# A weight chunk's split put behind the softmax pieces, and large VectorE pieces cut up

## The reference, cut to what matters

```python
for l in range(DEPTH):                       # DEPTH = 2
    shift, scale, gate = jnp.split(sc @ w_ada[l] + b_ada[l], 3, axis=-1)
    h = rms(x, norm_w[l]) * (1.0 + scale[:, None]) + shift[:, None]
    ...
    u = h @ w_in
    qa, ka, va, qb, kb, vb, cq, ckv, kpe, z = jnp.split(u, split_points(), axis=-1)
    ...                                      # rms of q and k per head, rotation of qb, kb
    o_a = natten_latent(qa, ka, va, ka_c, va_c, rpb_a[l])
    o_b = swa_latent(qb, kb, vb, kb_c, vb_c, sink_b[l])
    o_c = mla_latent(qc, kc, vc, kc_c, vc_c)
    x = x + gate[:, None] * merge_out(o_a, o_b, o_c, z, w_out[l])
```

## Time and profile before

| | |
|---|---|
| median of 3 runs | 3752.88 us (3751.07 to 3753.28) |
| profiled execution | 3745.93 us |
| its span | 3744.1 us |
| PE busy | 3560.6 us, 95% |
| DVE, ACT busy | 2012.7 us (54%), 1673.0 us (45%) |
| granted clock of TensorE, mean | 0.980 |
| loop of the change, layer 0 | about 269 to 717 us of the span |
| loop of the change, layer 1 | about 1390 to 1673 us |

### The profile page before, as it was taken

How to read it: one execution, slowest core, us unless ns; L and a number is a source line. 1 busy time by engine, 2 the same in 40 slices (tenths; PEclk the granted TensorE clock), 3 DMA queues, 4 the chain that set the end, 5 groups by cost and what they waited for, 6 DMA issues and landing times.

```text
span 3744.1 us, 46318 instructions
## 1 busy us (share of the span) xinstructions
PE 3560.6 (95%) x18672; PEld 2938.3 (78%) x18672; DVE 2012.7 (54%) x3121; ACT 1673.0 (45%) x2722; POOL 67.8 (2%) x118
## 2 busy tenths in 40 slices
PE   7899999999999899999999999999999799999998
PEld 2677778878777777788787777766788699999887
DVE  1676654345567756643354544445455566666544
ACT  2323344434422424455644435454545654444443
POOL 1200000000020000000000000000000000000000
PEclk8999999999999999999999999999999899999999
DMA  9653321133365565323365566635656265556665
GB/s 365 202 161 118 96 62 52 53 112 110 102 187 175 163 196 156 91 66 111 108 211 163 163 179 180 180 106 171 186 174 197 90 183 183 183 183 183 193 201 171
DMA packets 351045, 577.49 MB, mean 154 GB/s; under 512 B 25316, under 2 KB 131060, under 8 KB 348912
## 3 DMA queue, kind: packets, MB, share of 16 engines
q1 hardware_dynamic: 344512, 549.47, 47.6%
q0 software_dynamic: 6320, 25.06, 2.3%
HBM read 570.26 MB, written 4.19 MB: 153 GB/s over the span
## 4 chain that ended last, share of the span: by engine, by line
PE 57%; DVE 3%; ACT 3%; DMA 1%; issue 1%; DVEq 0%; SPq 0%; ACTq 0%
PE ps L711 36%; PE ps L1606 14%; PE ps L1288 2%; DMA raw_ring<-in_w_in_dram 1%; ACT w_hi L674 1%; DVE w_lo L680 1%; PE ps L1086 1%; PE ps L1200 1%; PE ps L1173 1%; PE ps L1182 1%; PE ps L748 0%; PE ps L1479 0%; PE ps L1484 0%; PE ps L1196 0%; DMA raw_ring<-in_w_proj_b_dram 0%
## 5 line engine op out<-in xcount | busy, mean ns | idle before, releaser
L680 DVE TENSOR_TENSOR w_lo<-raw_ring,w_hi 128x1024 fp32r<-128x1024 f32 (+1 forms) x827 | 1009.6, 1223 | 1097.0 <-ACT w_hi L674 1095.9
L674 ACT CAST w_hi<-raw_ring 128x1024 fp32r<-128x1024 f32 (+1 forms) x827 | 864.0, 1048 | 1241.1 <-PE ps L711 514.9
L711 PE MATMUL ps<-w_hi,r_a 128*128 128x512 f32 x3552 | 1286.5, 402 | 40.0 <-DVE w_lo L680 20.7
L711 PE MATMUL ps<-w_lo,r_a 128*128 128x512 f32 (+1 forms) x2624 | 1025.8, 391 | 0.0
L711 PE MATMUL ps<-w_hi,r_b 128*128 128x512 f32 (+1 forms) x2272 | 846.8, 392 | 9.1 <-issue 4.4
L711 PEld LDWEIGHTS ps<-w_hi,r_a 128*128 128x128 f32 x3552 | 674.9, 190 | 204.7 <-issue 36.9
L711 PEld LDWEIGHTS ps<-w_lo,r_a 128*128 128x128 f32 x2624 | 499.4, 190 | 102.8 <-issue 7.9
L711 PEld LDWEIGHTS ps<-w_hi,r_b 128*128 128x128 f32 x2272 | 432.4, 190 | 102.3 <-issue 4.7
L1606 PE MATMUL ps<-r_a,w_hi 128*128 128x256 f32 x2816 | 508.9, 284 | 0.0
L1606 PEld LDWEIGHTS ps<-r_a,w_hi 128*128 128x128 f32 x2816 | 440.8, 193 | 0.0
L1606 PE MATMUL ps<-r_a,w_lo 128*128 128x256 f32 x1408 | 399.4, 284 | 0.0
(11 more groups left out here) (338 smaller groups left out, 2939.1 us busy)
## 6 DMA issues: line engine op xcount, KB each, us to landing
raw_ring<-in_w_in_dram SPq DMA_DIRECT2D x386, 512.0 KB, 3.7
raw_ring<-in_ffn_w_up_dram SPq DMA_DIRECT2D x176, 512.0 KB, 3.5
raw_ring<-in_w_ada_dram SPq DMA_DIRECT2D x128, 512.0 KB, 3.9
raw_ring<-in_w_out_dram SPq DMA_DIRECT2D x96, 512.0 KB, 3.7
raw_ring<-in_ffn_w_down_dram SPq DMA_DIRECT2D x88, 512.0 KB, 4.3
gla_arena<-in_w_ada_dram SPq DMA_DIRECT2D x64, 512.0 KB, 8.4
raw_ring<-in_w_proj_b_dram SPq DMA_DIRECT2D x32, 512.0 KB, 3.6
raw_ring<-in_w_proj_a_dram SPq DMA_DIRECT2D x16, 512.0 KB, 3.6
```

The costliest lines, as they stand in the source:

```text
L674: nc.scalar.copy(WH[:, ph.s_slot(i, j), 0:n], RAW[:, ph.raw_slot(i, j), 0:n]).then_inc(hi_ready, 1)
L680: nc.vector.tensor_tensor(WL[:, ph.raw_slot(i, j), 0:n], RAW[:, ph.raw_slot(i, j), 0:n], WH[:, ph.s_slot(i, j), 0:n].bitcast(F32), ALU.sub ...
L711: mm = nc.tensor.matmul(PS[:, t, a:z], X(x, k, t), W[w][:, kk * cols + a:kk * cols + z], start=(k == 0 and q == 0), stop=(c == len(js) - 1 ...
```

## The change

No instruction is added or taken away; what moves is the order on ACT and DVE.

1. The split for chunk q+2 (`split` on ACT, `rest` on DVE) goes from the first part of chunk q, where it stood ahead of the part's other pieces, to its last part, behind them. `full` names the last part.
2. `u_evac` and `z_evac` evict the tiles of each part with that part of c = 7, and on ACT ahead of the split.
3. `u_sums` takes two tiles with each of the two parts of the next block's c = 0 (one tile with each part of `kpe`).
4. `b_rope` is cut in ten pieces (`ROPES`), one for each part of c = 2 to 6 of block 5; the wait that stood ahead of the first rotation goes to c = 2, with one more.

```diff
+        def full(l, name, b):
+
+            return {"win": WT[l][b], "kpe": KT, "z": 4 if l == 0 else 2}[name]
...
-                def u_evac(b):
-                    for t in range(WT[l][b]):
+                def u_evac(b, tiles=None):
+                    for t in tiles or range(WT[l][b]):
...
                 def weights(name, b, c, lo, hi):
-                    if name != "kt" and lo == 0:
+                    if name == "win" and c == 7:
+                        u_evac(b, range(lo, hi))
+                    if name == "z":
+                        if (c, lo) == (1, 0):
+                            root(f"uc{l}", RI[:, :, 32:34], RI[:, :, 32:34])
+                        if c == 7:
+                            z_evac(0, range(lo, hi))
+                    if name != "kt" and hi == full(l, name, b):
                         split(place_of(name, b, c) + 2)
                     if name == "win":
                         if (b, c, lo) == (5, 2, 0):
                             root(f"ub{l}", RI[:, :, 16:32], RI[:, :, 16:32])
-                        if c == 7 and hi == WT[l][b]:
-                            u_evac(b)
...
-                def u_sums(b):
+                def u_sums(b, tiles=None):
 
                     sq = SQA if b < 6 else SQB
-                    for t in range(WT[l][b]):
+                    for t in tiles or range(WT[l][b]):
...
-                def b_rope(t):
-
-                    for o, n, tab, w in ((QB, 8, 0, 0), (QB + 512, 4, 0, 2), (KB, 4, 1, 2)):
+                def b_rope(t, n0):
+
+                    for o, n, tab, w in ((QB, 8, 0, 0), (QB + 512, 4, 0, 2), (KB, 4, 1, 2))[n0]:
...
+                ROPES = ([(t, slice(k, k + 1)) for t in range(2) for k in range(3)]
+                         + [(t, k) for t in (2, 3) for k in (slice(0, 1), slice(1, 3))])
...
                     if name == "win":
                         for n, ci, kk in halves[b, c, lo]:
                             dve_ada(dve, n, ci, ACC["win"], (kk,))
-                    if name != "kt" and lo == 0:
+                        if c == 0 and b > 3:
+                            k = WT[l][b - 1] // (WT[l][b] // 2)
+                            u_sums(b - 1, range(lo // 2 * k, lo // 2 * k + k))
+                        if (b, c, lo) == (5, 1, 0):
+                            head_eps(f"ub{l}", 16, QB)
+                        if (b, c, lo) == (5, 2, 0):
+                            dve.wait_ge(acc_free, AC[win][4][0] + WT[l][4])
+                            dve.wait_ge(stage_ready, 6 * l + 4)
+                        if (b, c, lo) == (5, 3, 0):
+                            head_rinv(f"ub{l}", 16, 32)
+                        if b == 5 and 2 <= c < 7:
+                            b_rope(*ROPES[2 * (c - 2) + lo // 2])
+                    if name != "kt" and hi == full(l, name, b):
                         rest(place_of(name, b, c) + 2)
-                    if name == "win" and lo == 0:
-                        if c == 0 and b > 3:
-                            u_sums(b - 1)
...
-                        if b == 5 and 3 <= c < 7:
-                            b_rope(c - 3)
-                    elif name == "kpe" and lo == 0:
-                        u_sums(7)
-                    elif name == "z":
+                    if name == "kpe":
+                        u_sums(7, range(lo // 4, lo // 4 + 1))
+                    if name == "z":
...
-                        if c == 7 and hi == T:
-                            z_evac(0)
+                        if c == 7:
+                            z_evac(0, range(lo, hi))
```

More of the change, by code:

```diff
@@ L1852, in turned_qb, with z_evac @@
                         ins.then_inc(qk_ready, 1)
-                def z_evac(b):
+                def z_evac(b, tiles=None):
                     tmp = TMPZ if b == 0 else TMPC
-                    for t in range(T):
+                    for t in tiles or range(T):
                         a = 16 * l + b * T + t
@@ L1894, in weights @@
                         copies(TRN[f"kpe{l}"][0], kpe)
-                    else:
-                        if (c, lo) == (1, 0):
-                            root(f"uc{l}", RI[:, :, 32:34], RI[:, :, 32:34])
-                        if lo == 0 and 3 <= c < 7:
-                            latents(c - 3)
-                        if c == 7 and hi == T:
-                            z_evac(0)
+                    elif lo == 0 and 3 <= c < 7:
+                        latents(c - 3)
                 last = None
@@ L2684, in weights @@
                             dve_ada(dve, n, ci, ACC["win"], (kk,))
-                    if name != "kt" and lo == 0:
-                        rest(place_of(name, b, c) + 2)
-                    if name == "win" and lo == 0:
-                        if c == 0 and b > 3:
-                            u_sums(b - 1)
-                        if (b, c) == (5, 1):
-                            head_eps(f"ub{l}", 16, QB)
-                        if (b, c) == (5, 3):
-                            head_rinv(f"ub{l}", 16, 32)
-                            dve.wait_ge(acc_free, AC[win][4][0] + WT[l][4])
-                        if b == 5 and 3 <= c < 7:
-                            b_rope(c - 3)
-                    elif name == "kpe" and lo == 0:
-                        u_sums(7)
-                    elif name == "z":
+                        if c == 0 and b > 3:
[11 more added lines that the diff above has]
+                    if name != "kt" and hi == full(l, name, b):
+                        rest(place_of(name, b, c) + 2)
+                    if name == "kpe":
+                        u_sums(7, range(lo // 4, lo // 4 + 1))
+                    if name == "z":
                         if (c, lo) == (0, 0):
```

## The result

The changed kernel takes 3717.32 us (median of 4 runs, 3712.96 to 3718.61) against 3751.98 us; the ratio is 0.9909, with a 95% interval of 0.9895 to 0.9923: 34 us or 0.9% faster (28.9 to 39.4). Timed once more, beside another set of runs of the kernel before, it was 3718.41 us and 0.9903.

The account below looks back on a forecast made before the run. PE bounds the kernel, busy 3560.6 of 3744.1 us, losing time in waits in blocks 3 to 5. Layer 0's 18.2 and layer 1's 8.2 us make 26.4 off: 3726.5 us against the median of 3752.9; 8-in-10 range 3718 to 3742.

Parts of the forecast that it names:

- What bounds the kernel: PE is busy 3560.6 of 3744.1 us; the loss lies in its waits in blocks 3 to 5 of layer 0.
- The split moved: Layer 0: the cast comes a part later, so waits for late transfers go, for ACT and DVE behind it: 6.8 us.
- rival A: Casts find transfers as late as before; only the smaller pieces help, 12.9 us, so 3740 us; chance 0.15.
- The sums and rotations: Layer 0: with pieces cut, waits behind sums (4.6 us) and the first rotation (2.92 us) go.
- The sum: Both loops: 18.2 us from layer 0 and 8.2 from layer 1, 26.4 us off, giving 3726.5 us against the median.
- Sum for waits in layer 0: Layer 0's loop: PE's waits that go, 14.3 + 0.9 + 0.5 - 0.4 = 15.3 us.
- the three places named: Layer 0, behind block 5, block 7 and `kpe`'s last sum: casts behind evictions cost 0.7 us each, 2.1 us.
- The clock: Layer 0: three stretches at half clock behind waits go with them, 1.65 us each, 5.0 us.
- B: Rival: DVE has the same work, so waits only go to other places; 3745 to 3758 us; chance 0.08.
- C: Rival: evictions ahead of the split delay exponentials at twelve block or `kpe` ends; slower, 3762 us; chance 0.05.
- at best: Forecast's best case: all layer 0 waits, layer 1's 5.9 us and all slow stretches go: 31.5 us, so 3721.
- The sentence on slow matmuls: Slow matmuls vary from run to run, so the clock's share could be nothing, leaving 18.7 of 26.4 us.

Follow-up runs that it names:

- e5: Kernel before, all pieces in their old places, but the chunk split is q+1 instead of q+2, giving transfers a chunk more time; 3720.22 us, ratio 0.9913.
- e3: Changed kernel with the split behind the other pieces of the chunk's first part instead of its last; 3737.67 us, ratio 0.9962.
- e1: Kernel before with only the split moved to the chunk's last part; sums, rotations and evictions as before; 3713.31 us, ratio 0.9898.
- e2: Changed kernel with the split back in its old place, ahead of the first part's pieces, leaving the pieces alone; 3735.11 us, ratio 0.9961.
- e8: Changed kernel with 2 to 9 added ACT copies ahead of six exponentials in blocks 6 and 7 of layer 0; 3727.1 us in a single run.
- e4: Changed kernel with ACT's cast ahead of the evictions in a block's last part instead of behind them; 3715.90 us, ratio 0.9906.
- e9: Changed kernel with, in layer 0 alone, the cast ahead of the evictions and block 7's sums whole; 3715.67 us, ratio 0.9907.
- e6: Changed kernel with the split put off until behind the next step's largest value, exponential and scaled output; 3715.21 us, ratio 0.9889.

## Why the prediction missed its range

*What bounds the kernel* held: the loops' gain lies where PE waited in blocks 3 to 5, and e5 shows with every place left alone that late transfers made the values late.

*The split moved* held in its result and not in one reason. I said that the landing wait goes for ACT too; the casts still wait 21.0 us. What goes is what stood behind them: the largest value that the split held up now comes ahead of it, and the one that stands behind it now isn't due yet. DVE's waits for the casts fell from 52.9 to 14.1 us, and what is left of them reaches PE in one wait of 0.3 us. e3, with the split behind the pieces of the first part, shows that this needs the later part. So the prediction's own sign of rival A, casts that still wait 2 to 4 us, appeared with the gain all there: a cast's wait costs nothing where no value that is due stands behind it.

*The sums and rotations* were mis-assigned: 4.6 and 2.9 us were put down to their size. e1 has them whole and no wait; e5 shows that the sums' waits were landings, and the rotation's was 2.3 us of cast and subtraction ahead of 4.76 us of rotation. Either moving the split or cutting the piece ends that one (e1, e2). The total was not hurt by it, since each wait was counted once and the change did both; that is luck, not understanding.

*The sum* is where it failed, at "Sum for waits in layer 0: 15.3 us", less "2.1 us" for what it costs: the waits were priced at the idle time shown. e8 gives 0.22 us more for each. In layer 0 the kernel before has nine waits of PE more than the changed one, 2.0 us, and in layer 1 five, 1.1 us. The net idle time that went in layer 0 is 14.0 us (19.6 to 5.6 us over the loop), against 15.3 - 2.1 = 13.2; the costs, 1.4 at the three places named, were put 0.7 too high. The clock gave 4.6 us in three steps (1.4, 1.6, 1.6: what they lost above wait and 0.22) against 5.0. So 20.6 against 18.2. In layer 1 idle time fell by 6.5 us (5.5 said) and the 0.22s are 1.1; what is left of the 10.2 us, 2.6, is the clock's, whose slow time there fell from 10.2 to 3.4 us (2.65 said).

| us | said | measured |
|---|---|---|
| layer 0, net idle | 13.2 | 14.0 |
| layer 0, clock | 5.0 | 4.6 |
| layer 0, unshown part of a wait | 0 | 2.0 |
| layer 1 | 8.2 | 10.2 |
| both loops | 26.4 | 30.9 |

The medians have 34.7 us, 3.8 more than the loops. That lies within their interval (28.9 to 39.4), and the untouched rest of the span varies by 8 us from profile to profile; whether the kernel before loses more in its loops in other executions than in the one profiled was not tried. So of the 8.3 us by which the forecast was short, 3.1 are the unshown part of fourteen waits, 1.4 the other terms in sum, and 3.8 stay open. The bound of the range failed with the first: "at best" 31.5 us took idle times as the most that could come back; with 3.1 more it would have held the measured time, and the forecast itself would still lie 6 us above it.

*The rivals.* A, landing waits that stay, is wrong as a forecast, and its price, that of the pieces alone, came near by luck: 12.9 us said, 14.6 measured (e2) and 9.3 in the loops, where the sums gave 1.9 us for 2.5 and new waits for modulation work took 2.6 back. B falls: the waits did not go elsewhere. C falls by e4. The sentence on slow matmuls that vary from run to run could not be seen in its two rows, which are of one run. Two profiles of the changed kernel have 6.8 us of slow time in the loops both times, but 125 and 131 us over the span. From kernel to kernel the loops' slow time does not follow the waits: e9, whose order in layer 1 is that of the changed kernel, was slow for 6.8 us around a wait of 2.21 us at the start of that loop (first row), and the changed kernel, with the same wait, was not (second row). And e4 was slow in block 3 with no wait of TensorE in the 18 us before (third row):

```profile
1367.50:1374.30 6.80, 6.03 (x18) 5.00 (x19) 4.45 (x7) 2.56 (x4) 0.00 (x0) 0.50 0.33 122
```

```profile
1364.80:1371.60 6.80, 5.97 (x30) 5.09 (x31) 4.52 (x7) 2.68 (x4) 0.00 (x0) 1.00 0.52 165
```

```profile
286.80:290.00 3.20, 3.20 (x9) 2.43 (x9) 0.71 (x2) 0.00 (x0) 0.00 (x0) 0.50 0.15 54
```

## What to carry to other kernels

Where a small piece that the critical engine needs now stands in a queue behind a large one that waits for memory, move the large one behind it, but not past its own use: that alone brought the whole gain, cutting the other pieces up brought nothing on top, and a further step's delay (e6) brought new waits for the large one. Giving the transfer a chunk more time with every piece in its place (e5) came close to the same gain. Before cutting a piece, ask which of the work ahead of it is idle time; a run that only gives the transfer more time tells the two apart. Count a wait of TensorE with what its first instructions lose as well, and compare stretches between the same two instructions, since the rest of a span varies more than most edits bring.

## What the runs showed of the hardware that was not expected

An idle time shown ahead of a turn understates the wait by 0.22 us, in all four added waits at the full clock: 0.16 since a matmul's end is modelled later than the next could have started, 0.06 since the first transposes behind a wait come 0.17 us apart, not 0.11. And the clock follows no single wait: it stayed at 1.00 behind added waits of 0.28 to 1.58 us and behind 2.24 us in the kernel before, fell to 0.50 behind 2.32, and behind the added 3.21 and 4.18 us, for 6.8 us each; and around the same wait of 2.21 us it fell in e9 and stayed in the changed kernel.
